# Output-projection pieces, decode tokens and the value projection of the memory, reordered in a two-layer hybrid decoder step

## The chip, the cores and the metric

The kernel runs on one core of one Trainium2 chip. The metric is the device time of one execution in microseconds. The median of three runs before the change is 2929.29 us (2924.08, 2929.29 and 9859.3).

## The reference, cut to what matters

Two layers, each for 1024 prompt tokens and for 8 samples of 4 new tokens (32 decode tokens, 4096 cached positions per sample). All in float32.

```
u, cq, ckv, kpe, gq, gk, gv, ga, go = split(rmsnorm(x) @ w_in)
ya = pool_mixer(u)                                   # 256 columns of the mix
yb = mla_attend(q_lat, q_pe, ckv, kpe) @ w_uv        # 512: prompt causal; decode over pages + new tokens
# GLA, chunk by chunk, 4 heads, key width 32, value width 64
S  = exp(b_last) * S + einsum('bhsk,bhsv->bhkv', kb * exp(b_last - b), vb)   # one state per sample and head
yc = rmsnorm(o, g_gla) * silu(go)                    # 256
x  = x + concat(ya, yb, yc) @ w_out
mem_n = rmsnorm(mem_prompt, g_mem); mk = mem_n @ w_xk; mv = mem_n @ w_xv     # 256 memory tokens
x  = x + cross_attn(rmsnorm(x, g_x), mk, mv)
x  = x + hier_moe(rmsnorm(x, g_ffn))
```

The outputs are the activations, the new latents and keys, the pool buffers, the GLA states of the prompt and of each sample (head by head, so only the blocks of 32 x 64 in which a head's keys meet the same head's values), and mk and mv.

## The kernel before

The five engines run programs of their own, written out by hand in one order each, and meet through semaphores; nothing is scheduled. x lies feature-major in SBUF: 8 tiles of 128 features by 1056 tokens (1024 + 32), worked on in three chunks of 352 tokens. A layer is a sequence of stages with a barrier of four engines behind each (`stage_end`, L433): 2 (input projection, pool, MLA of the prompt), 3 (GLA), 4 (decode attention over the cached pages), 5 (output projection), 9 (cross attention and routing), then the experts and the sum of their outputs. A float32 matmul leaves two records in the trace.

**GLA (stage 3).** Prompt chunks of 128 tokens, n = 0 to 7. On TensorE, `levels(n)` (L882, small matmuls into banks 0 to 3) waits until DVE has taken chunk n-1 out of those banks and GpSimd has made the factors; then come `turn_kt`, `outputs` and `states` of the chunk before. DVE's `take_levels` is seven predicated copies (L1987) and one product; then it adds the state (L2009, a product with the block mask, and L2010), takes the output, begins chunk n+2 (a scan and seven subtractions, L1973 and L1977), and for odd n norms two chunks (`norm_o`, L2001 to L2005). ScalarE takes exponentials for chunk n+2 and the roots of the norms (`roots_of`); exponential and root are in different tables, and each change is an ACT_TABLE_LOAD.

**Pieces.** `part(i)` (L928) is a piece of the output projection that needs no GLA output: the first 6 of 8 contraction tiles of output tile j, chunk c, from `PART`, into bank 5, which DVE's `add_part` adds to x. Chunk 2 holds decode tokens and is left out. PART has five of the eight such pieces. The three others are done whole in the gaps at the end of stage 4 by `project` (L1021, 8 matmuls each, at L1086, L1095 and L1113).

**Decode tokens of GLA.** Behind the loop DVE norms the last two prompt chunks, then prepares the 32 decode tokens (L2048 to L2071, with ScalarE's exponentials L1572 to L1575 between). TensorE then makes their attention (L956), outputs (L966, L968) and eight states (L977), which alternate between banks 7 and 5; DVE adds each by two instructions, a product with the block mask (`bdmask`) and the update.

**Decode attention (stage 4).** At its start TensorE multiplies queries with the keys of the new tokens (L988 to L992: a transpose and 16 small matmuls), DVE takes their maxima (L2100 to L2107) and ScalarE the exponential (L1600). Then sample by sample: GpSimd gathers the cache rows into three slots; TensorE transposes them four blocks at a time through banks 0 and 1, which ScalarE (L1591) and DVE (L2113) empty in turn, and makes scores (L1031, L1038); DVE takes the maximum (L2118), ScalarE the exponential (L1596); the probabilities are transposed and multiplied with the values (L1055) inside the next sample. Behind sample 7 stands a chain of small steps that puts the shares together (L1090 to L1116).

**Stage 5 and behind.** `linear` (L666) runs the output projection, DVE adds each tile to x (L2180), ScalarE squares it (L1399), DVE sums the squares (L2188). Behind the barrier: the sum over partitions (L656), ScalarE's roots (L1405), DVE's norm (L1791, L1793); meanwhile TensorE projects the memory to values (L1136) and keys (L1143), and then makes the queries (L666 again).

## Time and profile before

| | |
|---|---|
| median of the runs | 2929.29 us |
| the profiled execution's own time | 2909.44 us |
| its span | 2907.6 us |
| PE busy (matmul records) | 2629.3 us, 90% |
| DVE, ACT, POOL busy | 1181.6, 721.1, 413.6 us |
| chain: PE, DVE, ACT | 80%, 11%, 4% |
| L935, first and second layer, records | 120 |
| stage 3, first layer | about 437 to 549 us |
| stage 4 | 549 to 692 us |
| stage 5 | 692.5 to 782 us |

Busy time counts an engine's instructions, overlapped or not with others. The chain is followed back from the last instruction to what released it, so that only its members can shorten the run. In a timeline row the two first numbers are the start and the length of a group in microseconds, x is the number of records, and a bracket gives the idle time of the engine ahead of it and what ended it. Where a clock is given, 1.00 is TensorE at 2.4 GHz and 0.50 at 1.2 GHz.

### The profile page before, as it was taken

The numbers are of one execution on the slowest core, as the hardware profiler recorded it, in microseconds if no ns is written. First come the engines' busy times: TensorE is split into PE (matmuls) and PEld (weight loads), VectorE is DVE, ScalarE is ACT, GpSimd is POOL, SyncE is SP. The second block draws the span as 40 slices with busy tenths as digits, with TensorE's granted clock in tenths as the row PEclk, the third lists the DMA queues.
The fourth block names the chain that finished last, engine by engine and source line by source line (L and its number), as shares of the span: only waits on it lengthen the run. The fifth ranks groups of instructions, "written<-read, shape, count | busy, mean of one in ns | idle before, by whom it ended". The sixth has DMA issues, their size and how long they took to land.

```text
span 2907.6 us, 39018 instructions
## 1 busy us (share of the span) xinstructions
PE 2629.3 (90%) x15964; PEld 1837.8 (63%) x15964; DVE 1181.6 (41%) x2218; ACT 721.1 (25%) x1448; POOL 413.6 (14%) x561
## 2 busy tenths in 40 slices
PE   7999987899999979999699999788999997999993
PEld 4645556556567568888465455565666665888872
DVE  4155558442313433232352555574323234323325
ACT  1124453331003301111301344443211132111113
POOL 0004216110000011111100223241000000111111
PEclk9999997799999989999799999968999997999996
DMA  4001001342042268898510100114222313889854
GB/s 160 17 17 32 6 4 34 116 179 73 29 137 98 99 223 325 323 336 321 193 38 4 37 11 8 34 38 152 106 87 98 108 44 139 307 317 334 331 211 181
DMA packets 76933, 385.65 MB, mean 133 GB/s; under 512 B 25087, under 2 KB 31869, under 8 KB 65725
## 3 DMA queue, kind: packets, MB, share of 16 engines
q1 hardware_dynamic: 53164, 304.90, 28.8%
q0 software_dynamic: 23040, 76.59, 7.5%
q8 instruction: 100, 1.64, 0.2%
q10 hardware_dynamic: 576, 2.10, 0.2%
q14 instruction: 53, 0.43, 0.0%
HBM read 355.55 MB, written 44.55 MB: 138 GB/s over the span
## 4 chain that ended last, share of the span: by engine, by line
PE 80%; DVE 11%; ACT 4%; DMA 1%; issue 1%; POOLq 1%; POOL 1%; SPq 0%; DVEq 0%; ACTq 0%
PE ps L666 17%; PE ps L1314 16%; PE ps L1327 8%; PE ps L1232 4%; PE ps L724 4%; PE ps L804 4%; PE ps L816 2%; PE ps L1000 2%; PE ps L832 2%; PE ps L1303 2%; PE ps L782 2%; DVE arena L1987 2%; PE ps L1025 1%; PE ps L1038 1%; DVE nmax L1888 1%
## 5 line engine op out<-in xcount | busy, mean ns | idle before, releaser
L666 PE MATMUL ps<-arena,ring 128*128 128x352 f32 x1704 | 505.8, 459 | 3.4 <-DVE arena L1777 2.4
L1314 PEld LDWEIGHTS ps<-arena 128*128 128x128 f32 x4096 | 470.4, 193 | 35.7 <-issue 35.7
L1314 PE MATMUL ps<-arena 128*128 128x104 f32 x4096 | 470.0, 276 | 4.9 <-issue 2.5
L666 PEld LDWEIGHTS ps<-arena,ring 128*128 128x128 f32 x1704 | 323.4, 190 | 183.6 <-issue 3.5
L1327 PE MATMUL ps<-arena 128*104 128x512 f32 x512 | 230.4, 593 | 2.6 <-ACT arena L1707 2.6
L1707 ACT ACTIVATE arena<-ps 104x1024 f32<-104x1024 f32 x64 | 65.6, 1024 | 470.7 <-PE ps L1327 470.7
L2408 DVE TENSOR_SCALAR arena<-arena 128x208 f32<-128x208 f32 x64 | 17.2, 269 | 400.8 <-ACT arena L1700 400.8
L2543 POOL DMA_INDIRECT arena<-xrow,arena x64 | 70.5, 1102 | 671.8 <-PE ps L1303 353.2
L1327 PEld LDWEIGHTS ps<-arena 128*104 128x104 f32 x512 | 81.9, 170 | 103.9 <-issue 103.9
L804 PE MATMUL ps<-arena 96*128 96x512 f32 (+3 forms) x384 | 146.1, 490 | 0.0
L1232 PE MATMUL ps<-arena,ring 128*128 128x352 f32 x384 | 117.7, 463 | 1.6 <-DVE arena L2258 1.6
L1476 ACT ACTIVATE ring<-ps 128x512 f32<-128x512 f32 (+2 forms) x192 | 87.3, 490 | 124.8 <-PE ps L816 124.7
L1000 PE MATMUL ps<-consts,arena 128*128 128x128 f32 x640 | 99.5, 295 | 19.0 <-ACT arena L1591 12.7
L724 PE MATMUL ps<-arena 128*128 128x512 f32 x256 | 111.2, 593 | 4.5 <-ACT arena L1427 4.5
L816 PE MATMUL ps<-consts,ring 128*128 128x128 f32 x576 | 89.7, 283 | 24.7 <-DVE arena L1899 9.7
L1481 ACT ACTIVATE ring<-ps,nmax 128x128 f32<-128x128 f32 (+7 forms) x128 | 94.6, 741 | 53.5 <-DVE nmax L1889 52.9
L1000 PEld LDWEIGHTS ps<-consts,arena 128*128 128x128 f32 x640 | 74.3, 148 | 49.0 <-ACT arena L1591 23.9
L2549 POOL DMA_INDIRECT yrow<-arena x64 | 65.2, 1018 | 266.7 <-ACT arena L1707 252.5
L1232 PEld LDWEIGHTS ps<-arena,ring 128*128 128x128 f32 x384 | 71.7, 190 | 46.1 <-issue 6.8
L816 PEld LDWEIGHTS ps<-consts,ring 128*128 128x128 f32 x576 | 64.2, 142 | 57.2 <-issue 33.9
L1888 DVE TENSOR_REDUCE nmax<-ps 128x1 f32<-128x128 f32 (+7 forms) x128 | 97.0, 758 | 4.4
L1887 DVE TENSOR_TENSOR ps<-ps,consts 128x128 f32<-128x128 f32 x128 | 38.3, 299 | 146.3 <-PE ps L804 145.4
(410 smaller groups left out, 3649.1 us busy)
## 6 DMA issues: line engine op xcount, KB each, us to landing
arena<-in_w_e SPq DMA_DIRECT2D x64, 3072.0 KB, 13.8
ring<-in_ring SPq DMA_DIRECT2D x56, 512.0 KB, 3.5
arena<-yrow SPq DMA_DIRECT2D x16, 1024.0 KB, 7.9
arena<-in_mem_k SPq DMA_DIRECT2D x16, 512.0 KB, 6.4
arena<-in_mem_v SPq DMA_DIRECT2D x16, 512.0 KB, 10.0
xrow<-arena SPq DMA_DIRECT2D x16, 512.0 KB, 6.4
x<-in_x SPq DMA_DIRECT2D x3, 1408.0 KB, 11.8
out_y<-arena SPq DMA_DIRECT2D x3, 1408.0 KB, 5.6
```

The source lines that it names most:

```text
L666: mm = pe.matmul(ps[:, (j % 2) * NCH + c, 0:CH], ring[:, j // per, (j % per) * units + k, :], src[:, k, tok], start=k == k0, stop=k == uni ...
L724: mm = pe.matmul(ps[:, 6 + t % 2, :], xn[:, k, t * P:t * P + m], wvg[:, k, :], start=k == 0, stop=k == KT - 1)
L804: mm = pe.matmul(ps[:, bank + at // 512, 0:end - at], q_h[0:QK, b, qb * P:(qb + 1) * P], k_h[0:QK, b, at:end], start=True, stop=True)
L816: mm = pe.transpose(ps[:, bank, (kb % 4) * P:(kb % 4 + 1) * P], prob[:, e, kb * P:(kb + 1) * P], ident)
L1000: mm = pe.transpose(ps[:, turn_bank(u), j * P:(j + 1) * P], b, ident)
L1232: mm = pe.matmul(ps[:, (j % 2) * NCH + c, 0:CH], ring[:, slot, (j % 2) * XH + k, :], co[:, k, tok], start=k == 0, stop=k == XH - 1)
L1314: mm = pe.matmul((gate_ps if m < 2 else up_ps)[:, m % 2, 0:rows], w_e[j][:, at:at + P], xb_t[:, p, k, 0:rows], start=k == 0, stop=k == KT - 1)
L1327: mm = pe.matmul(ps[0:rows, 4 + f, :], h_t[:, p, k, 0:rows], w_e[j][:, at:at + 512], start=k == 0, stop=k == 1)
L1476: act.activation(pt[:, e, 512 * half:512 * half + w], ps[:, 4 + m % 2, 0:w], ACT.Copy).then_inc(tp_free[m % 2], 1)
L1481: act.activation(prob[:, e, 0:w], ps[:, 2 * e:2 * e + 2, :].rearrange("p a n -> p (a n)")[:, 0:w], ACT.Exp, bias=nmax[:, e, 1:2], scale=ML ...
L1888: step(dve.reduce_max(nmax[:, e, 0:1], sc, AX))
L2543: pool.indirect_dma_start(xb[0:rows, n % 2, :], None, xrow, bass.IndirectOffsetOnAxis(ap=idx[0:rows, 0, n:n + 1], axis=0), bounds_check=TO ...
```

## The change

Six edits, made in each layer:

- PART has eight pieces instead of five. Their place in the loop is behind `states(n)` for n = 1 to 5; the last stands behind the loop. `project` in stage 4 starts at contraction tile 6.
- The eight decode states use six banks in turn, and DVE adds each by one instruction, without the product with the block mask. What then stands outside the heads' blocks is not read by anything.
- DVE's two last norms stand behind the decode tokens' preparation, and ScalarE's root for them behind the decode exponentials.
- The new tokens' scores (`new_scores`), their maxima (`new_maxima`) and exponential move from the start of stage 4 behind sample 0's scores, into sample 1.
- The value projection of the memory moves from behind the sums of squares to ahead of barrier 5.
- TensorE's wait for the new tokens' maxima (`tail_dve` at 3) moves ahead of the transposes of sample 0's probabilities.

```diff
-PART = ((1, 1), (2, 0), (2, 1), (3, 0), (3, 1))
+PART = ((1, 1), (1, 0), (2, 0), (2, 1), (3, 0), (3, 1), (0, 0), (0, 1))
 PART_K = 6
+STATE_BANKS = (7, 5, 0, 1, 2, 3)
...
                     states(n)
-                    if n in (1, 3):
-                        part(2 + n // 2)
+                    if 1 <= n <= len(PART) - 3:
+                        part(1 + n)
...
-                part(4)
+                part(len(PART) - 1)
...
-                    if b >= 2:
-                        pe.wait_ge(st_ready, NT + 1 + b - 1)
-                    pe.matmul(ps[:, 7 - 2 * (b % 2), 0:GW], d_kt[0:ND, b, :], vg[0:ND, NT, 0:GW],
+                    if b >= len(STATE_BANKS):
+                        pe.wait_ge(st_ready, NT + 1 + b + 1 - len(STATE_BANKS))
+                    pe.matmul(ps[:, STATE_BANKS[b % len(STATE_BANKS)], 0:GW], d_kt[0:ND, b, :], vg[0:ND, NT, 0:GW],
...
-                pe.wait_ge(tail_dve, 1)
-                pe.transpose(ps[:, 3, 0:P], ckv_rep.rearrange("p r k -> p (r k)"), ident).then_inc(tail_pe, 1)
-                for n in range(DB):
...
+                def new_scores():
+
+                    pe.wait_ge(tail_dve, 1)
+                    pe.transpose(ps[:, 3, 0:P], ckv_rep.rearrange("p r k -> p (r k)"), ident).then_inc(tail_pe, 1)
+                    for n in range(DB):
+                        out = ps[0:ND, 7, n * ND:(n + 1) * ND]
+                        pe.matmul(out, q_dec[:, n, :], ckv_new, start=True, stop=False)
+                        mm = pe.matmul(out, qpe_new[64:96, n, :], kr_new[64:96, :], start=False, stop=True)
+                    mm.then_inc(tail_pe, 1)
...
-                    for k in range(KT):
-                        pe.matmul(ps[:, j * NCH + c, 0:CH], ring[:, j, k, :], mix[:, k, chunks[c][1]], start=k == 0, stop=k == KT - 1)
+                    for k in range(PART_K, KT):
+                        pe.matmul(ps[:, j * NCH + c, 0:CH], ring[:, j, k, :], mix[:, k, chunks[c][1]], start=k == PART_K, stop=k == KT - 1)
...
+                    if n == 1:
+                        pe.wait_ge(tail_dve, 3)
                     if n >= 1:
                         up = u
                         turn_probs(n - 1, up)
...
                     rope_scores(n, 1, False).then_inc(sc_done, 1)
+                    if n == 0:
+                        new_scores()
...
                 linear(1, IN_MT + RING, 3, mix)
-                stage_end(pe, 5)
-
-                pe.wait_ge(sq_added, 1)
-                sum_squares(lambda k, c: sq[:, 0, chunks[c][1]], None, 1, NCH, 0, sq_ready, ssq_ready)
                 pe.wait_ge(mnorm_ready, 1)
                 pe.wait_ge(wxv_full, 16)
                 for t in range(2):
...
                     mm.then_inc(mv_done, 1)
+                stage_end(pe, 5)
+
+                pe.wait_ge(sq_added, 1)
+                sum_squares(lambda k, c: sq[:, 0, chunks[c][1]], None, 1, NCH, 0, sq_ready, ssq_ready)
...
-                roots_of(P, 2)
                 act.wait_ge(g_sub, NT + 1)
...
                 act.activation(g_last[:, 0, :], g_b[:, 0, 0:ND].rearrange("p (b t) -> p b t", b=DB)[:, :, DT - 1], ACT.Exp).then_inc(g_exp, 1)
+                roots_of(P, 2)
...
                         take_turn(u, ct[:, h, 0:4, :].rearrange("p b k -> p (b k)"))
+                        if h == 0 and n == 1:
+                            act.wait_ge(tail_dve, 3)
+                            act.activation(p_new[0:ND], p_new[0:ND], ACT.Exp, scale=MLA_SCALE).then_inc(pd_ready, 1)
                         if h == 0 and n >= 1:
                             probs(n - 1)
...
-                    if n in (2, 4):
-                        add_part(1 + n // 2)
+                    if 2 <= n <= len(PART) - 2:
+                        add_part(n)
...
                 take_o(NT - 1)
-                norm_o(NT - 2, P)
-                norm_o(NT - 1, P)
...
-                add_part(4)
+                add_part(len(PART) - 1)
+                norm_o(NT - 2, P)
+                norm_o(NT - 1, P)
...
                     dve.wait_ge(st_done, NT + b + 1)
-                    dve.wait_ge(st_ready, NT + b + 1)
-                    add_state(d_state[:, b, :], 7 - 2 * (b % 2), g_last[:, 0, b:b + 1])
+                    dve.scalar_tensor_tensor(out=d_state[:, b, :], in0=d_state[:, b, :], scalar=g_last[:, 0, b:b + 1],
+                                             in1=ps[:, STATE_BANKS[b % len(STATE_BANKS)], 0:GW], op0=ALU.mult,
+                                             op1=ALU.add).then_inc(st_ready, 1)
...
                     if n >= 1:
                         maxima(n - 1)
+                    if n == 1:
+                        new_maxima()
```

How the order of instructions changes is shown at three places; the line numbers of the changed kernel are 1 to 5 higher. On TensorE in the GLA loop, behind a chunk without a piece before (L893 is `levels`, L907 to L909 `outputs`, L916 `states`, L935 a piece):

```order
L893 MATMUL ps<-arena 128x64 x28
L894 MATMUL ps<-consts,arena 128x4
L900 MATMUL ps<-consts,arena 128x128
L907 MATMUL ps<-arena 128x256
L909 MATMUL ps<-arena 128x64 x4
L916 MATMUL ps<-arena 128x256
L893 MATMUL ps<-arena 128x64 x28
```

and in the change:

```order
L894 MATMUL ps<-arena 128x64 x28
L895 MATMUL ps<-consts,arena 128x4
L901 MATMUL ps<-consts,arena 128x128
L908 MATMUL ps<-arena 128x256
L910 MATMUL ps<-arena 128x64 x4
L917 MATMUL ps<-arena 128x256
L936 MATMUL ps<-arena,ring 128x352 x6
L894 MATMUL ps<-arena 128x64 x28
```

A piece stands between the states of one chunk and the levels of the next but one. On TensorE at the start of stage 4 before (L988 and L991, L992 are the new tokens' scores, cut after two of eight pairs in what follows):

```order
L982 MATMUL ps<-consts,arena 128x32 x2
L988 MATMUL ps<-consts,arena 128x128
L991 MATMUL ps<-arena 32x32
L992 MATMUL ps<-arena 32x32
L991 MATMUL ps<-arena 32x32
L992 MATMUL ps<-arena 32x32
```

and in the change, up to the same matmuls:

```order
L983 MATMUL ps<-consts,arena 128x32 x2
L1003 MATMUL ps<-consts,arena 128x128 x16
L1014 MATMUL ps<-consts,arena 128x128 x4
L1003 MATMUL ps<-consts,arena 128x128 x16
L1014 MATMUL ps<-consts,arena 128x128 x4
L1041 MATMUL ps<-arena 128x512
L1034 MATMUL ps<-arena 32x512 x8
L1041 MATMUL ps<-arena 128x512
L991 MATMUL ps<-consts,arena 128x128
L994 MATMUL ps<-arena 32x32
L995 MATMUL ps<-arena 32x32
```

All transposes and scores of sample 0 stand ahead of them now. On TensorE behind decode attention before:

```order
L1025 MATMUL ps<-arena,ring 128x352 x8
L1116 MATMUL ps<-arena 64x32 x8
L666 MATMUL ps<-arena,ring 128x352 x42
L1125 MATMUL ps<-arena,consts 128x256 x8
L666 MATMUL ps<-arena,ring 128x352 x96
L656 MATMUL ps<-arena,consts 128x352 x3
L1136 MATMUL ps<-arena 128x512 x16
L1143 MATMUL ps<-arena,ring 128x256 x32
```

and in the change:

```order
L1028 MATMUL ps<-arena,ring 128x352 x2
L1121 MATMUL ps<-arena 64x32 x8
L667 MATMUL ps<-arena,ring 128x352 x42
L1130 MATMUL ps<-arena,consts 128x256 x8
L667 MATMUL ps<-arena,ring 128x352 x96
L1137 MATMUL ps<-arena 128x512 x16
L657 MATMUL ps<-arena,consts 128x352 x3
L1148 MATMUL ps<-arena,ring 128x256 x32
```

The last block of `project` has two matmuls instead of eight, the output projection keeps its 42 and 96, and the values (L1136, now L1137) stand ahead of the sums of squares (L656, now L657).

## Rows read from the trace of the kernel before

**Rows 1.** The page's chain of waits: share of the span by engine.

```profile
PE 80%; DVE 11%; ACT 4%; DMA 1%; issue 1%; POOLq 1%; POOL 1%; SPq 0%; DVEq 0%; ACTq 0%
```

**Rows 2.** Table by stretches: us, busy (records) per engine, clock, DMA share, GB/s.

```profile
437.00:549.00 112.00, 86.83 (x693) 64.83 (x693) 83.87 (x227) 38.32 (x146) 50.19 (x141) 0.71 0.13 46
...
563.00:564.00 1.00, 1.00 (x10) 1.00 (x10) 0.30 (x1) 0.60 (x1) 0.00 (x0) 0.89 0.88 377
```

**Rows 3.** Timeline of PE in the GLA stage: start, us, what, idle before.

```profile
474.23 1.79 PE L893 MATMUL ps<-arena 32*128 32x64 f32 x56
...
499.94 3.26 PE L893 MATMUL ps<-arena 32*128 32x64 f32 x56 [3.78 <-POOL arena L2505]
...
522.41 3.72 PE L935 MATMUL ps<-arena,ring 128*128 128x352 f32 x12
...
533.74 4.69 PE L966 MATMUL ps<-arena 128*32 128x256 f32 x16
```

**Rows 4.** Timeline of PE, second layer, the decode tokens' first matmuls.

```profile
1957.79 1.49 PE L956 MATMUL ps<-arena 128*32 128x128 f32 x6 [4.92 <-DVE arena L2071]
```

**Rows 5.** Timeline of DVE, the end of the GLA stage.

```profile
512.53 3.83 DVE L1987 COPY_PREDICATED arena<-lmask,ps 128x256 f32<-128x256 uint8 x7 [2.78 <-PE ps L894]
...
525.16 0.18 DVE L2001 RECIPROCAL arena<-arena 128x4 f32<-128x4 f32 x1 [1.95 <-ACT arena L1545]
...
527.18 0.17 DVE L2048 COPY arena<-arena 128x32 f32<-128x32 f32 x1
...
532.59 0.28 DVE L2076 TENSOR_TENSOR arena<-ps,consts 32x128 f32<-32x128 f32 x1 [1.15 <-PE ps L956]
...
548.55 0.48 DVE L2010 SCALAR_TENSOR_TENSOR arena<-arena 128x256 f32<-128x256 f32 x1
```

**Rows 6.** Timeline of ScalarE, decode tokens, and decode attention's start.

```profile
528.59 0.26 ACT L1572 ACTIVATE arena<-arena 128x64 f32<-128x64 f32 x1 [2.15 <-DVE arena L2059]
...
555.30 1.28 ACT L1600 ACT_TABLE_LOAD   x1 [6.73 <-DVE arena L2107]
...
569.35 1.12 ACT L1596 ACTIVATE arena<-ps,arena 128x1024 f32<-128x1024 f32 x1 [0.42 <-DVE arena L2119]
```

**Rows 7.** Timeline of PE, the start of decode attention.

```profile
549.54 0.44 PE L988 MATMUL ps<-consts,arena 128*128 128x128 f32 x1 [1.33 <-DVE arena L2100]
...
557.54 1.97 PE L1000 MATMUL ps<-consts,arena 128*128 128x128 f32 x8 [1.76 <-ACT arena L1591]
...
567.70 1.04 PE L1000 MATMUL ps<-consts,arena 128*128 128x128 f32 x8
...
571.19 1.06 PE L1000 MATMUL ps<-consts,arena 128*128 128x128 f32 x8
...
580.93 1.04 PE L1000 MATMUL ps<-consts,arena 128*128 128x128 f32 x8
```

**Rows 8.** GpSimd's load for sample 1, and DMA issues from 549 to 570.

```profile
553.10 0.94 POOL L2514 DMA_INDIRECT arena<-in_cache_ckv,page_i  x1 [37.22 <-DMA out_gla_s<-arena]
...
arena<-in_cache_ckv,page_i POOLq DMA_INDIRECT x2, 10.4
```

**Rows 9.** Timeline of PE, end of decode attention, start of the output projection.

```profile
660.26 4.90 PE L1025 MATMUL ps<-arena,ring 128*128 128x352 f32 x16
...
683.50 7.96 PE L1025 MATMUL ps<-arena,ring 128*128 128x352 f32 x16
...
692.54 25.12 PE L666 MATMUL ps<-arena,ring 128*128 128x352 f32 x84 [0.49 <-ACTq L435]
```

**Rows 10.** PE behind the output projection, and DVE's last norm there.

```profile
781.89 3.59 PE L656 MATMUL ps<-arena,consts 128*128 128x352 f32 x6 [3.99 <-DVEq L435]
785.32 13.90 PE L1136 MATMUL ps<-arena 128*128 128x512 f32 x32
...
812.86 22.35 PE L666 MATMUL ps<-arena,ring 128*128 128x352 f32 x75
...
799.16 4.06 DVE L1793 SCALAR_TENSOR_TENSOR arena<-x,vec,arena 128x352 f32<-128x352 f32 x8
```

More of the change, by code:

```diff
@@ L984, in _ @@
                 stage_end(pe, 3)
-                pe.wait_ge(tail_dve, 1)
-                pe.transpose(ps[:, 3, 0:P], ckv_rep.rearrange("p r k -> p (r k)"), ident).then_inc(tail_pe, 1)
-                for n in range(DB):
-                    out = ps[0:ND, 7, n * ND:(n + 1) * ND]
-                    pe.matmul(out, q_dec[:, n, :], ckv_new, start=True, stop=False)
-                    mm = pe.matmul(out, qpe_new[64:96, n, :], kr_new[64:96, :], start=False, stop=True)
-                mm.then_inc(tail_pe, 1)
+                def new_scores():
[6 more added lines that the diff above has]
+                    mm.then_inc(tail_pe, 1)
                 def ring_turns(u, blocks):
@@ L1075, in _ @@
                     latent_scores(n, 0, False)
-                    if n == 1:
-                        pe.wait_ge(tail_dve, 3)
                     if n >= 1:
@@ L2089, in _ @@
                 for b in range(DB):
-                    if b == 3:
+                    if b == 5:
                         norm_o(NT, ND)
                     dve.wait_ge(st_done, NT + b + 1)
-                    dve.wait_ge(st_ready, NT + b + 1)
-                    add_state(d_state[:, b, :], 7 - 2 * (b % 2), g_last[:, 0, b:b + 1])
+                    dve.scalar_tensor_tensor(out=d_state[:, b, :], in0=d_state[:, b, :], scalar=g_last[:, 0, b:b + 1],
+                                             in1=ps[:, STATE_BANKS[b % len(STATE_BANKS)], 0:GW], op0=ALU.mult,
+                                             op1=ALU.add).then_inc(st_ready, 1)
                 step.sync()
@@ L2100, in _, with new_maxima @@
                 dve.tensor_copy(ckv_rep, ckv_new.unsqueeze(1).broadcast_to([P, 4, ND])).then_inc(tail_dve, 1)
-                dve.wait_ge(tail_pe, 1)
-                dve.tensor_copy(ckv_tok, ps[:, 3, 0:P]).then_inc(tail_dve, 1)
-                dve.wait_ge(tail_pe, 2)
-                step(dve.tensor_tensor(p_new[0:ND], ps[0:ND, 7, 0:DB * ND].rearrange("p (b k) -> p b k", b=DB),
-                                       con("newmask", ND).rearrange("p (b k) -> p b k", b=DB), ALU.add))
-                step(dve.tensor_reduce(m_new[0:ND, :], p_new[0:ND], AX, ALU.max))
-                dve.tensor_tensor(p_new[0:ND], p_new[0:ND], m_new[0:ND, :].unsqueeze(2).broadcast_to([ND, DB, ND]),
-                                  ALU.subtract).then_inc(tail_dve, 1)
+                def new_maxima():
+                    dve.wait_ge(tail_pe, 1)
+                    dve.tensor_copy(ckv_tok, ps[:, 3, 0:P]).then_inc(tail_dve, 1)
+                    dve.wait_ge(tail_pe, 2)
+                    step(dve.tensor_tensor(p_new[0:ND], ps[0:ND, 7, 0:DB * ND].rearrange("p (b k) -> p b k", b=DB),
+                                           con("newmask", ND).rearrange("p (b k) -> p b k", b=DB), ALU.add))
+                    step(dve.tensor_reduce(m_new[0:ND, :], p_new[0:ND], AX, ALU.max))
+                    dve.tensor_tensor(p_new[0:ND], p_new[0:ND], m_new[0:ND, :].unsqueeze(2).broadcast_to([ND, DB, ND]),
+                                      ALU.subtract).then_inc(tail_dve, 1)
                 def take_turn(u, dst):
```

2 lines of the change are left out of this document (removed).

## Prediction

> **What bounds the kernel now.** I began with the page: TensorE (PE) holds 80% of the chain that ended last and DVE 11% [rows 1], so a microsecond is won only where PE waits, or where PE does work on the chain that could stand in one of its waits. Then I took a table by stretches and the timeline of each engine around the moved pieces. The GLA stage (437 to 549 us) keeps PE busy for 86.83 of its 112 us, at a mean clock of 0.71 of full speed [rows 2]: room for more matmuls. The reader should see two prices of the same instructions: 56 small records take 1.79 us at the high clock and 3.26 us at the low one [rows 3]. (A matmul leaves two records in the trace, so a piece of six matmuls is x12.) The second layer repeats the first 1426.73 us later: its wait of 4.92 us ahead of L956 [rows 4] has the place and the size of the first layer's. So I cost one layer and double it.
>
> **1. Three more pieces in the GLA loop.** Each is x12 records, 3.72 us at the high clock [rows 3]; before, they were the first six of eight matmuls in the three blocks at L1025. Piece 1+n now stands behind states(n), for n = 1 to 5, and its bank is free only once DVE has added the piece before it, at the end of DVE's own step n. So a piece starts just as DVE begins its seven predicated copies (3.83 us [rows 5]), during which PE has nothing else to do, since levels(n+2) waits for those copies and the bias product behind them. 3.72 us beside 3.83 + 0.42 us: hidden, at the high clock. At the low clock a piece takes some 7 us and shows 2.7 us past the cover. What the pieces fill is the gap of 3.78 us ahead of levels(6) [rows 3], and fuller work should keep the clock up, which is worth 1.5 us at levels(7), for which DVE waits 2.78 us [rows 5]. The three extra adds on DVE (0.5 us each) stand ahead of that wait. I take -0.5 us; ends -2 and +9.
>
> **2. The decode tokens' end of the GLA stage.** DVE was free at 525.16 - 1.95 = 523.2 us but prepared the decode tokens only at 527.18, after two norms [rows 5]. Now it starts at 523.2. ScalarE had its table loaded by 528.59 - 2.15 = 526.4 and then waited 2.15 us for DVE [rows 6]; that wait goes, and the decode products come 2.2 us earlier. The norms (2.0 us for two, from 525.16 to 527.18) now stand behind them, ahead of the read at 532.59, which had 1.15 us of idle time: that read comes 2.2 - 2.0 + 1.15 = 1.3 us earlier. Then the eight states. Before, DVE did sixteen operations and a norm from 539.0 to 549.0, in step with PE over two banks. Now eight operations of 0.48 us [rows 5], a norm of 1.0 and PE's sixteen records, which at 0.29 to 0.43 us each (4.69 us for sixteen of this width between the two clocks [rows 3]) take 4.7 to 6.9 us: 6.4 us in place of 10.0. Together -1.3 - 3.6 = -4.9 us; ends -3 and -6.
>
> **3. The new tokens' scores, from the start of decode attention to behind sample 0.** They occupy PE from 549.54 to 557.54 - 1.76 - 1.97 = 553.81 us, that is 4.3 us, and behind them ScalarE's table load and exponential hold up its first copy by 1.6 us (from 555.30 to 556.9, the end of PE's wait at 557.54 less the copy's own 0.6) [rows 6, 7]. Both go: -5.9 us. But sample 1 gets them back. Between its first transpose (567.70) and the transposes of sample 0's probabilities (571.19) lie 3.5 us now [rows 7]. After the change this is 4.3 us of small matmuls, 1.5 us of DVE (553.81 to 555.30), 1.6 us of table load and exponential, and the 1.8 us from ScalarE's large exponential at 569.35 to 571.19 [rows 6]: 9.2 us, +5.7. Nothing covers it, since DVE's and ScalarE's copies of sample 1 are queued behind those waits. Besides, the tiny matmuls and the wait should drop the clock, as the 32-column matmuls of step 4 do, behind which dense ones start at the low clock; eight transpose records take 1.97 us low against 1.06 high [rows 7], so 4 us of dense work at the low clock cost 2 us more. The cover on the other side is thin as well: sample 1's cache rows are asked for at 553.10 and take 10.4 us to land [rows 8], 563.5 at best, while PE will want them some 0.2 + 12.3 + 4.3 us after the stage's start, at 566. Sum +2 us; ends -1 and +6.
>
> The same row on table loads bears on a page. The trace shows 1.28 us and the exponential right behind it [rows 6]. The Trainium skill ("ScalarE: Activation LUTs", What ACT_TABLE_LOAD costs) adds a drain and gives about 2.66 us for each switch; by that, sample 1 would lose 1.4 us more in each layer. The trace disagrees, and I keep its number.
>
> **4. The end of decode attention.** The blocks at L1025 shrink from x16 to x4. The first (4.90 us at 660.26) covered DVE's maximum and ScalarE's exponential; at sample 0 that exponential starts 1.65 us behind the last scores' records and takes 1.3 [rows 6, 7], so the next PE work is ready at about 663.2 instead of 665.0: -1.8. The second, as long, becomes 1.2: the copy it covers is ready by then, -3.6. The third (683.50) takes 7.96 us, which is eleven records at the low price of 0.587 and five at the high one of 0.293: four cost 2.35, -5.6 [rows 9]. Against these: before, this block brought the clock back 6.5 us in, so that the output projection at 692.54 ran at 0.30 us a record from its first one (25.12 us for x84 [rows 9]). Now it starts some 3.5 us after 683.5 and runs low for 3 to 6 us: +2.3, with the ends 1.5 and 3.3. The small matmuls ahead may be cold for longer: +0.5. Sum -8.2 us; ends -11 and -5. The projection itself has as many matmuls as before.
>
> **5. The value projection ahead of the barrier.** PE idles 3.99 us there while DVE adds the last tile and two squares, then runs the sums of squares at the low clock, 3.59 us for x6 [rows 10]; at 0.293 a record they need 1.8. With the 13.90 us of values in front, the others finish first, and PE passes the barrier in about the 0.49 us that the last one took [rows 9]: -3.5 - 1.8. What the values covered is uncovered: the roots on ScalarE, 0.7 us of wait ahead of the key projection, and DVE's norm, which now ends behind the barrier by the same 19 us, at about 812. The key projection (14 us) covers its first chunks, and the query projection wants the third chunk only after four tiles of 4.7 us. DVE ended at 803.2 before, with PE ready for it at 812.9: a slack of 10 us, and enough is left [rows 10]. Sum -4.6 us; ends -5.8 and -3.
>
> **The sum.** -0.5 - 4.9 + 2.0 - 8.2 - 4.6 = -16.2 us a layer, -32 for both. The profiled execution's own time is 2909.4 us (span 2907.6), so its like would be 2877. The runs' median lies 20 us above it, at 2929.3 (two runs within 5 us of each other, the third an outlier): I forecast 2897 us.
>
> **The rivals.**
> (a) *The pieces run at the low clock* and each of the four behind the second shows 3 us past DVE's copies: +12.5 us a layer, 2922 us. For it: levels(6) at 499.94 already runs low [rows 3]. Against: each piece is the densest work there is in the loop. 0.12.
> (b) *Sample 1 lengthens more*: the low clock lasts over all of it, and its cache rows land late. A sample lasts 13.2 us at the high clock (567.70 to 580.93, the same for the next ones); at the transposes' ratio of 1.97 to 1.06 it would take 10 us more, so +8 on my term: 2913 us. 0.10.
> (c) *The clock stays high through the GLA stage*, and the decode tokens' end gains by it too: every term at its better end gives -26 a layer, 2878 us. 0.10.
> (d) *The clock does not come back in decode attention*: slower. All but the first samples cost 10 us more each, and beyond 1.6 samples a layer at the low clock the gain is gone; with seven it is -16 + 70 a layer, some 3037 us. For it would speak that transposes come first in each sample. Against: between 553.81 and 563.9 PE did nothing but transposes, and the clock rose in 563 to 564 (0.89 [rows 2]). 0.02. The Trainium skill ("TensorE: Matmul & The Clock Gate", Part 4: PE-mode transpose) says that transposes do not count as busy for the clock; the trace here disagrees, as that rise shows.
> My forecast has the other 0.66. That the moves are undone by another order is no case: the order of instructions shows each of them.
>
> **How the numbers follow.** The range 2866 to 2918 holds the forecast with its terms between the ends, (b) and (c), and allows for runs at the profiled level instead of 20 us above it; (d) and part of (a) are outside. Faster by over 2% (about what a measurement can tell from no change) means below 2870.7: only (c) on a good run, 0.05. Slower by over 2% is (d), 0.02. Within 2%: 0.93.
>
> **What would show it.** Right, in the changed profile: the last set of predicated copies of a layer's loop starting no later than 512.5; the stage's end near 544; PE transposing at once in the next stage, then a wait of 4 us or more in sample 1 released by ScalarE, at a clock below 1.00; blocks of x4; the sums of squares at 1.8 us behind a gap under 1 us. Wrong: predicated copies waiting for PE in each step of the GLA loop (step 1), a gap at sample 1 ended by a DMA (step 3), the output projection taking over 29 us for its x84 (step 4), or a wait for DVE at the query projection (step 5).

## The result and the profile after

| | before | changed |
|---|---|---|
| median of the runs shown, us | 2926.68 (4 runs, one an outlier of 9859) | 2875.54 (4 runs, 2866.96 to 2883.03) |
| profiled execution's own time, us | 2909.44 | 2866.96 |
| its span, us; mean granted clock | 2907.6; 0.94 | 2865.1; 0.952 |
| PE busy (matmul records), us | 2629.3 | 2605.3 |

The ratio is 0.9834, 95% interval [0.9801, 0.9868]: 1.7% faster, within the 2% called no change. A second set of runs on one chip gave 0.9848 [0.9823, 0.9874]. The forecast was 2897; the range 2866 to 2918 held the result, but the gain was larger than its sum.

A ledger of both layers comes first. Each column is the time between two starts on TensorE's timeline: first piece of the GLA stage, first cache transposes of decode attention, first shortened block at its end (L1025 before, L1028 now), output projection's first tile, memory's squares, query projection.

| us, layer 1 / layer 2 | before | changed | difference |
|---|---|---|---|
| A first piece to transposes | 112.5 / 112.7 | 101.4 / 101.6 | -11.1 / -11.1 |
| B transposes to end block | 106.5 / 106.5 | 108.9 / 108.1 | +2.5 / +1.6 |
| C end block to output projection | 32.3 / 32.3 | 22.0 / 21.8 | -10.3 / -10.5 |
| D first tiles of the projection | 25.0 / 25.0 | 27.6 / 25.0 | +2.7 / 0.0 |
| E memory's squares to queries | 95.4 / 95.4 | 90.9 / 90.9 | -4.5 / -4.5 |
| sum | 371.6 / 371.8 | 350.8 / 347.3 | -20.8 / -24.5 |

The two sums give 45.2 us, and the spans differ by 42.5: everything outside these stretches takes 2164.3 us before and 2167.0 after. So the gain is where the edits are.

The table by stretches shows the clock [rows 2]. Columns: stretch, its length, busy us and records of PE, PEld, DVE, ACT and POOL, granted clock, DMA share, GB/s.

```profile
443.75:545.00 101.25, 85.53 (x729) 61.90 (x729) 77.32 (x206) 36.79 (x143) 46.59 (x139) 0.85 0.13 42
545.00:549.00 4.00, 3.87 (x20) 3.40 (x21) 1.17 (x4) 1.19 (x2) 0.00 (x0) 0.58 0.31 66
549.00:555.00 6.00, 5.87 (x41) 3.05 (x40) 2.45 (x4) 1.79 (x3) 3.75 (x4) 1.00 0.72 254
...
559.00:563.00 4.00, 3.51 (x16) 3.05 (x17) 1.74 (x4) 2.33 (x4) 0.00 (x0) 0.50 0.96 409
```

The GLA stage has a mean clock of 0.85, where the same stretch (441.30 to 549.17) had 0.72. The clock falls to 0.50 as decode attention starts and is at 1.00 from 549 us on; taken by single microseconds the clock came back 3.2 us after the first transposes. Before, those started at 553.81 and it came in 563 to 564, 9.4 us after them.

PE in the GLA loop, answering to [rows 3]: the pieces behind states(2) to states(5), of which the first, third and fourth stand where there was none before, and levels(6):

```profile
480.35 3.71 PE L936 MATMUL ps<-arena,ring 128*128 128x352 f32 x12
...
489.12 3.79 PE L936 MATMUL ps<-arena,ring 128*128 128x352 f32 x12 [0.53 <-DVE x L2023]
...
498.69 3.71 PE L936 MATMUL ps<-arena,ring 128*128 128x352 f32 x12
502.65 1.79 PE L894 MATMUL ps<-arena 32*128 32x64 f32 x56 [0.24 <-POOL arena L2516]
...
507.62 3.79 PE L936 MATMUL ps<-arena,ring 128*128 128x352 f32 x12 [0.53 <-DVE x L2023]
```

levels(6) waits 0.24 us instead of 3.78 and runs at the high clock. DVE's timeline at the end of the stage [rows 5], the last row being the first of the next stage:

```profile
513.99 3.84 DVE L1993 COPY_PREDICATED arena<-lmask,ps 128x256 f32<-128x256 uint8 x7 [0.67 <-PE ps L895]
...
524.60 0.17 DVE L2052 COPY arena<-arena 128x32 f32<-128x32 f32 x1
...
532.59 0.27 DVE L2082 TENSOR_TENSOR arena<-ps,consts 32x128 f32<-32x128 f32 x1
...
540.68 2.21 DVE L2099 SCALAR_TENSOR_TENSOR arena<-arena,ps 128x256 f32<-128x256 f32 x5 [0.21 <-PE ps L978]
...
545.16 0.23 DVE L2107 COPY arena<-arena 128x128 f32<-128x128 f32 x1
```

and ScalarE's, for the decode tokens' exponentials [rows 6]:

```profile
526.52 1.28 ACT L1576 ACT_TABLE_LOAD   x1
527.81 0.26 ACT L1576 ACTIVATE arena<-arena 128x64 f32<-128x64 f32 x1
```

The stage began 2.45 us later here (443.75 for 441.30), so from its start the copies come 1.0 us earlier, the read of the products 2.45, and L2107 6.46. Five states go through in 2.21 us without a wait between them. That they are five comes of an edit which the list of changes leaves out: the decode tokens' own norm moved from behind the third state to behind the fifth. It belongs to the decode tokens' part, and no run separates it from the states. The exponential now follows its table load at once.

PE in decode attention [rows 7]:

```profile
545.13 3.61 PE L1003 MATMUL ps<-consts,arena 128*128 128x128 f32 x16 [0.91 <-DVEq L436]
...
549.01 2.60 PE L1003 MATMUL ps<-consts,arena 128*128 128x128 f32 x16
...
555.66 0.27 PE L991 MATMUL ps<-consts,arena 128*128 128x128 f32 x1
555.86 0.25 PE L994 MATMUL ps<-arena 128*32 128x32 f32 x2
556.04 0.24 PE L995 MATMUL ps<-arena 32*32 32x32 f32 x2
...
559.49 3.87 PE L1003 MATMUL ps<-consts,arena 128*128 128x128 f32 x16 [0.70 <-DMA arena<-in_cache_kpe,page_i]
...
564.67 1.41 PE L1003 MATMUL ps<-consts,arena 128*128 128x128 f32 x8 [0.46 <-ACT arena L1596]
```

Sample 0 has no wait and lasts 10.5 us; the new scores (555.66) take 3.1 us at the high clock; sample 1 then meets its cache rows 0.70 us before they land. ScalarE there:

```profile
560.64 0.60 ACT L1596 ACTIVATE arena<-ps 128x512 f32<-128x512 f32 x1 [7.95 <-PE ps L1003]
561.25 1.28 ACT L1610 ACT_TABLE_LOAD   x1
562.55 0.41 ACT L1610 ACTIVATE arena<-arena 32x256 f32<-32x256 f32 x1
562.87 1.09 ACT L1601 ACTIVATE arena<-ps,arena 128x1024 f32<-128x1024 f32 x1
```

PE at the end of decode attention and at barrier 5 [rows 9, 10]; the row at 2081.21 is the second layer's projection:

```profile
654.06 1.35 PE L1028 MATMUL ps<-arena,ring 128*128 128x352 f32 x4
656.97 0.27 PE L1095 MATMUL ps<-consts,arena 128*8 128x128 f32 x1 [1.56 <-ACT arena L1601]
...
658.54 1.35 PE L1028 MATMUL ps<-arena,ring 128*128 128x352 f32 x4
...
671.81 2.71 PE L1028 MATMUL ps<-arena,ring 128*128 128x352 f32 x4
...
676.01 27.80 PE L667 MATMUL ps<-arena,ring 128*128 128x352 f32 x84 [0.49 <-ACTq L436]
...
763.90 13.90 PE L1137 MATMUL ps<-arena 128*128 128x512 f32 x32
778.06 2.01 PE L657 MATMUL ps<-arena,consts 128*128 128x352 f32 x6 [0.26 <-PEq L436]
780.63 14.08 PE L1148 MATMUL ps<-arena,ring 128*128 128x256 f32 x64 [0.55 <-ACT arena L1410]
...
2081.21 25.12 PE L667 MATMUL ps<-arena,ring 128*128 128x352 f32 x84 [0.49 <-ACTq L436]
```

### The profile page after: what moved, and what is told of

It reads as the page before. It is cut to its first block, busy times and chain, and to the rows that moved or that the text cites. A ratio compares the mean times of both kernels' runs of the same rounds, so it can differ in the third digit from the quotient of the medians.

```text
span 2865.1 us, 38998 instructions
## 1 busy us (share of the span) xinstructions
PE 2605.3 (91%) x15964; PEld 1817.8 (63%) x15964; DVE 1176.1 (41%) x2208; ACT 720.4 (25%) x1448; POOL 413.7 (14%) x561
## 4 chain that ended last, share of the span: by engine, by line
PE 73%; DVE 10%; PEld 4%; ACT 4%; issue 4%; DMA 2%; POOLq 1%; POOL 1%; PEldq 1%; SPq 0%; DVEq 0%; ACTq 0%
PE ps L1319 16%; PE ps L667 12%; PE ps L1332 8%; PE ps L1237 4%; PE ps L725 4%; PE ps L805 4%; PEld ps L667 4%; PE ps L817 2%; PE ps L833 2%; PE ps L1003 2%; PE ps L1308 2%; PE ps L783 2%; DVE arena L1993 1%; DVE nmax L1894 1%; PE ps L936 1%
## 5 line engine op out<-in xcount | busy, mean ns | idle before, releaser
L1003 PE MATMUL ps<-consts,arena 128*128 128x128 f32 x640 | 99.9, 296 | 18.7 <-ACT arena L1596 10.4
L1003 PEld LDWEIGHTS ps<-consts,arena 128*128 128x128 f32 x640 | 73.9, 149 | 48.6 <-ACT arena L1596 19.9
```

The costliest lines, as they stand in the source:

```text
L1003: mm = pe.transpose(ps[:, turn_bank(u), j * P:(j + 1) * P], b, ident)
```

## The experiments

Twelve runs followed, of eleven kernels, each against the kernel before on the same chip; the third column counts the two layers' sums of the ledger against before (743.3 us).

| kernel | ratio to before, 95% | ledger, us |
|---|---|---|
| e1_values: before + value projection | 0.9947 [0.9924, 0.9971] | -10.9 |
| e2_scores: before + scores' move | 0.9991 [0.9971, 1.001] | -5.2 |
| e3_pieces: before + eight pieces | 0.9943 [0.9923, 0.9962] | -16.0 |
| e4_decode: before + decode tokens | 0.9954 [0.9933, 0.9975] | -15.8 |
| c_change: the change again | 0.9848 [0.9823, 0.9874] | -43.5 |
| u2_no_scores: change less scores' move | 0.9888 [0.9864, 0.9913] | -40.3 |
| u3_no_pieces: change less pieces | 0.9900 [0.9882, 0.9918] | -27.8 |
| d1_norms: before + half of e4 | 0.9996 [0.9983, 1.001] | -6.2 |
| x_double: change, pieces twice | 0.9966 [0.995, 0.9982] | -16.1 |
| i1_preload: change + early table load | 0.9857 [0.9829, 0.9886] | -50.9 |
| i1_again: the same | 0.9848 [0.9827, 0.9868] | -51.0 |
| i2_late_scores: i1 + scores behind sample 2 | 0.9857 [0.9828, 0.9886] | -41.1 |

**My theory** was that each part saves in its own place and the savings add. **The rival** was that they gain from one another through TensorE's clock. Each part was done alone first, its code being its part of the change's diff.

*The value projection alone.*

```diff
-                stage_end(pe, 5)
-
-                pe.wait_ge(sq_added, 1)
-                sum_squares(lambda k, c: sq[:, 0, chunks[c][1]], None, 1, NCH, 0, sq_ready, ssq_ready)
                 pe.wait_ge(mnorm_ready, 1)
...
                     mm.then_inc(mv_done, 1)
+                stage_end(pe, 5)
```

> The kernel before with one part of the change alone: the value projection of the memory ahead of barrier 5. Theory (the parts save separately, each in its own place): of the changed kernel's profile the step from the last output-projection tile to the query projection is 4.3 us shorter per layer, so 8.6 us less in all, about 2921 against 2929 for the kernel before. The clock over the barrier stays as it is there. Rival (the value projection only fills a wait that the later work then shows again, because the keys wait for the norm of the memory or for the sum over the barrier): 0 to 3 us less in all, with a new idle time ahead of the key projection of 3 us or more.

Column E is 90.9 in both layers, -4.5, the whole of what the change has there; the rows are those of the change to 0.01 us (the sums 2.01 us behind 0.26 of waiting). No wait of 3 us appeared at the keys. The median fell by 15.9 us, more than 9: 1.7 us of the rest are in column C of the second layer, and what is left lies outside the ledger. The rival falls.

*The scores' move alone.*

```diff
-                pe.wait_ge(tail_dve, 1)
-                pe.transpose(ps[:, 3, 0:P], ckv_rep.rearrange("p r k -> p (r k)"), ident).then_inc(tail_pe, 1)
...
                     rope_scores(n, 1, False).then_inc(sc_done, 1)
+                    if n == 0:
+                        new_scores()
```

> The kernel before with the new tokens' scores moved into sample 1, and nothing else. Theory A (the clock rises some 4 us after the first transposes, whatever ran before them, as in the changed kernel): sample 0 lasts about 10.5 us instead of 18.5, sample 1 about 19.1 instead of 13.2, so 2.1 us less per layer and 4 us less in all. Theory B (TensorE's sparse work at the end of the GLA stage, which this kernel keeps, holds the clock down longer, about 10 us after the first transposes as in the kernel before): sample 0 lasts 12.6 us or more, so that the edit alone gives nothing or loses up to 2 us per layer: 0 to 4 us more in all, and the gain in the changed kernel came from the two edits together.

Theory A, with the clock of the stage's first eight microseconds as witness:

```profile
548.75:552.75 4.00, 4.00 (x18) 3.53 (x19) 1.02 (x3) 1.20 (x2) 0.05 (x1) 0.50 0.31 66
552.75:556.75 4.00, 3.75 (x26) 2.78 (x24) 2.67 (x4) 1.79 (x3) 3.09 (x4) 0.96 0.61 188
```

The GLA stage ends here as sparsely as before, and still the clock is up 4.3 us after the first transposes (3.9 in the second layer). A and B together are 1.9 and 1.4 us shorter; the rest of the 5.2 is clock in column C (-3.0 and -1.5), against +1.1 and +1.4 in E, where the value projection starts low behind the barrier. The interval holds 1.

*The pieces alone.*

```diff
-PART = ((1, 1), (2, 0), (2, 1), (3, 0), (3, 1))
+PART = ((1, 1), (1, 0), (2, 0), (2, 1), (3, 0), (3, 1), (0, 0), (0, 1))
```

> The kernel before with eight pieces of the output projection in the GLA loop instead of five, and the tail of decode attention shortened by their work; nothing else. Theory (as separate savings): the loop no longer than before (added pieces 3.7 us each, in waits that were there), the tail and the first tile of the output projection about 8 us shorter per layer, 16 us less in all, and the output projection runs cold at its start (2.7 us more in one layer, as in the changed kernel). Rival (the loop gets longer by what the pieces take, 3 times 3.7 us at high clock, and its wait only moves): the tail's gain is eaten by 5 to 11 us per layer, 0 to 8 us less in all. Second rival (the loop is shorter only since the pieces hold the clock up): the loop is 1 us shorter here too, and the levels of turn 6 start at high clock.

In both layers column C is 11.7 us shorter, D 2.7 longer and E 1.2 longer, and column A is 0.3 and 0.5 us shorter: the sum is -16.0 as the theory had it. The second rival holds for its smaller part: levels(6) runs at the high clock (1.79 us) and the last copies come 0.7 us earlier. The mean clock of the stage is 0.82 here (443.24 to 555.00) for 0.72 before, and column A hardly shortens: in this stage TensorE's clock buys little.

*The decode tokens alone.*

```diff
-                    dve.wait_ge(st_ready, NT + b + 1)
-                    add_state(d_state[:, b, :], 7 - 2 * (b % 2), g_last[:, 0, b:b + 1])
+                    dve.scalar_tensor_tensor(out=d_state[:, b, :], in0=d_state[:, b, :], scalar=g_last[:, 0, b:b + 1],
+                                             in1=ps[:, STATE_BANKS[b % len(STATE_BANKS)], 0:GW], op0=ALU.mult,
+                                             op1=ALU.add).then_inc(st_ready, 1)
```

> The kernel before with the decode tokens' part of the GLA stage alone: states without the mask and in six banks, norms of the last two turns behind the decode tokens' factors. Theory (separate savings): the stage ends 5.4 us earlier per layer than before, 11 us less in all. In the stage behind it the clock of TensorE decides a further part: if sparse work at the end of the GLA stage held it down, it rises earlier here and sample 0 is up to 2 us shorter per layer (15 us less in all); if not, sample 0 keeps its 18.5 us. Rival (the norms that were moved become the last to end, so the stage's end is theirs): 1 to 2 us less per layer, 2 to 4 us less in all, with TensorE idle at the stage's end behind the norms.

Column A is 5.8 us shorter, as expected; B is unchanged (106.3), so sample 0 keeps its length; C gives 3.0 more by its clock, and E takes 1.1 back. The 15 us are there, but their second part comes at the other end of decode attention than expected. The rival (the norms end last) falls: DVE's last operations are states, as in the change.

The four ratios add up to 0.53 + 0.09 + 0.57 + 0.46 = 1.65% and the four ledgers to 47.9 us, against 1.52% (and 1.66% in the first set) and 43.5 to 45.2 us for the change.

> The changed kernel once more, with more runs, as the level for the others of this set. Theory (the four parts save separately): the four run alone gave ratios of 0.9947 (value projection), 0.9991 (scores), 0.9943 (pieces) and 0.9954 (decode tokens), which add up to 4.8% less... 0.53 + 0.09 + 0.57 + 0.46 = 1.65%, so a ratio of 0.9835 here, some 48 us less. Rival (they gain from one another through the clock of TensorE): a ratio under 0.980.

(The sum in that text is 1.65%; the "4.8%" in it is a slip for 48 us.) The theory stands: no gain from the parts' meeting is seen, though the intervals would hide one of some 10 us. Inside it the clock's shares do not add, but nearly cancel: the four alone sum to -18 us a layer in column C, where the change has -10, and to -1 in E, where it has -4.5.

*The scores' move, and then the pieces, taken out of the change.*

```diff
+                pe.wait_ge(tail_dve, 1)
+                pe.transpose(ps[:, 3, 0:P], ckv_rep.rearrange("p r k -> p (r k)"), ident).then_inc(tail_pe, 1)
...
-                    if n == 0:
-                        new_scores()
```

> The changed kernel with the new tokens' scores back at the start of decode attention (the other three parts stay). Theory A (the scores' move is worth what it is alone, 1.4 to 1.9 us per layer): 3 to 5 us more in all than the changed kernel; the sample-0 transposes again wait for ScalarE and the clock reaches its high level some 10 us after the first of them. Theory B (the move pays only since the GLA stage now ends at the high clock): here the scores themselves run at the high clock (0.25 us a pair of records, as they do in sample 1 of the changed kernel, instead of 0.32), so the front is 1 us shorter than in the kernel before and the change is worth less here, 0 to 2 us in all.

Ledger +0.6 and +2.6 us, 3.2 in all: the lower end of A (columns A and B alone +2.1 and +2.8). The ratio says more, 0.9888 for 0.9848, some 12 us, with intervals that overlap; what exceeds 3.2 lies outside the ledger and is not explained. The scores at the start run low (0.32 and 0.31 us a pair of records), and the clock comes 8.8 us after the first transposes, which again wait 1.8 us for ScalarE behind its table load. B falls.

```diff
-PART = ((1, 1), (1, 0), (2, 0), (2, 1), (3, 0), (3, 1), (0, 0), (0, 1))
+PART = ((1, 1), (2, 0), (2, 1), (3, 0), (3, 1))
```

> The changed kernel with five pieces instead of eight (the other three parts stay). Theory A (separate savings): 8 us per layer more than the changed kernel (the price that the pieces had alone), a ratio to the kernel before near 0.990, and the last step of the GLA stage at the high clock as in the changed kernel. Theory B (the pieces are what keeps the clock up, so the GLA stage ends at the low clock here): the end of the stage from the last output piece to its barrier is 1 to 2 us longer and the levels of turn 6 run low, but sample 0 of decode attention is as short as in the changed kernel, because its clock rises some 4 us after the first transposes either way: 9 to 10 us per layer more.

+6.0 and +9.8 us, 15.8 in all: A's size. One point of B is true, the levels without a piece ahead of them:

```profile
497.30 3.26 PE L894 MATMUL ps<-arena 32*128 32x64 f32 x56 [3.79 <-POOL arena L2516]
...
535.32 3.72 PE L978 MATMUL ps<-arena 32*128 32x256 f32 x16
```

The stage's last matmuls (535.32, 0.23 us a record) are at the high clock without the pieces as well. And column A is 101.9 and 102.0, only 0.4 longer: 1.47 us of clock on PE and 3.5 us of its waiting are nearly off the path, on which DVE's own work lies.

This run also prices the low clock in sample 1. In its first layer the clock does not fall behind the new scores at all, and column B is still 108.5 us, for 108.9 and 109.1 in the change's two profiles and 106.5 before:

```profile
555.17 1.09 PE L1003 MATMUL ps<-consts,arena 128*128 128x128 f32 x8 [1.14 <-DMA arena<-in_cache_kpe,page_i]
...
559.89 1.07 PE L1003 MATMUL ps<-consts,arena 128*128 128x128 f32 x8 [1.76 <-ACT arena L1596]
```

The transposes run high here, and TensorE waits 1.76 us for ScalarE where the change, at the low clock, waits 0.46.

*How full is the loop?*

```diff
-                    for k in range(PART_K):
+                    for k in tuple(range(PART_K)) * (2 if i >= 2 else 1):
```

> The changed kernel with the last six of the eight pieces computed twice (the second pass overwrites the first with the same values), so each takes 7.4 us instead of 3.7. Theory (a piece is hidden beside DVE's seven predicated copies and its add, 3.83 + 0.42 us, and no more): each of the five in the loop shows 3.2 us, and the last, with 2.34 us of waiting behind it, 1.4 us: 17 us per layer, 35 us in all. Rival (TensorE has slack left in the loop, so that the copies of DVE alone set its pace): under 2 us for each, under 20 us in all. Second rival (the full TensorE shortens nothing and delays ScalarE's and GpSimd's inputs as well): over 45 us in all.

The ratio is 1.18% above the change's, 34 us; the ledger has 11.1 and 16.4 us, of which A 10.5 and 14.4. One step:

```profile
488.53 7.26 PE L936 MATMUL ps<-arena,ring 128*128 128x352 f32 x24
...
500.03 7.26 PE L936 MATMUL ps<-arena,ring 128*128 128x352 f32 x24
```

From piece to piece the loop took 7.92, 8.77, 9.57, 8.93 and 16.39 us in the change (from 472.43, 480.35, 489.12, 498.69 and 507.62 on) and takes 11.07, 11.07, 11.50, 11.06 and 19.78 here (the rows are the third of these steps): of 3.5 us more, 3.2, 2.3, 1.9, 2.1 and 3.4 show. So the pieces nearly fill the cover, with a slack of 0.1 to 1.6 us in a step, which I had not counted. By the ratio the theory's 35 us is right, by the ledger, with 27.4, it is some 8 us too much; the 7 us between ratio and ledger are not explained.

*Half of the decode tokens' part: the order of the norms.*

```diff
-                norm_o(NT - 2, P)
-                norm_o(NT - 1, P)
...
                 add_part(4)
+                norm_o(NT - 2, P)
+                norm_o(NT - 1, P)
```

> The kernel before with one half of the decode tokens' part: the last two norms and their roots behind the decode tokens' factors, the states as before (masked, two banks). Theory (two separate terms, 1.3 us for the order and 3.6 to 4.2 us for the states, of the 5.4 to 6.0 us that both together gave): 1.3 us per layer less up to the start of decode attention, 3 us in all, within what the comparison can tell. Rival (the order gives nothing alone, since the states' chain of DVE and TensorE follows and hides it, or the roots' table load moves onto the path): 0 or up to 1 us more.

Column A -0.8 and -1.0; of the ledger's 6.2 us the rest is clock (it comes 7 us after the first transposes instead of 9.4, and earlier in C). The whole cannot be told from no change. The states' half, which did not run alone, is then worth 5.8 - 0.9 = 4.9 us a layer.

*Two tries to do better.* Both load ScalarE's table in its idle time at the start of decode attention; the second also moves the scores behind sample 2.

```diff
+                act.activation(st_e[0:DB, 0, 0:1], con("ones", DB)[:, 0:1], ACT.Exp)
                 u = 0
...
-                    if n == 0:
+                    if n == 2:
+                        pe.wait_ge(o_kept, 2)
                         new_scores()
```

> The changed kernel with one exponential of 32 values more, into a scratch place, at the start of ScalarE's decode attention, so that the table is loaded in its idle time ahead of sample 0 and not in sample 1. Theory (the load is on sample 1's path): sample 1 shorter by what TensorE waits there for ScalarE, at least the 0.46 us ahead of the second half's transposes, at most the 1.28 us of the load: 0.5 to 1.3 us per layer, 1 to 2.5 us in all. Rival (sample 1 is paced by TensorE at the low clock and by the cache rows, so the load is hidden behind them): nothing, under 0.3 us per layer.

> As the one with the early table load, and with the new tokens' scores behind sample 2 instead of sample 0 (their exponential in sample 3). Theory A (in sample 1 the small matmuls cost more than their own 3.1 us because the cache rows land just then, 0.70 us, and because the clock falls behind them, 1.5 to 2 us on the next transposes): behind sample 2 the rows are there, and the whole costs 3.1 us plus the maxima's wait: samples 0 to 3 together 1 to 2.5 us shorter per layer than in the changed kernel. Theory B (the clock falls behind 32-column matmuls wherever they stand, and the rows of sample 1 are waited for longer now that TensorE comes for them 3 us sooner): TensorE waits some 3.8 us for the rows ahead of sample 1 (0.70 + 3.1), and the fall of the clock behind the scores comes later: together equal or up to 4 us per layer longer.

> The changed kernel with the early table load once more, for its interval. Theory (the local saving of 3 to 4 us per layer between the GLA stage and the query projection is real, and the whole differed since other stages took their clock otherwise): a ratio of 0.982 to 0.984, against 0.985 for the changed kernel. Rival (the saving is given back): 0.985 or more.

i1, ScalarE at the start of the stage (the load stands where it waited 1.77 us before):

```profile
551.22 1.28 ACT L1604 ACT_TABLE_LOAD   x1
552.52 0.20 ACT L1604 ACTIVATE arena<-consts 8x1 f32<-8x1 f32 x1
552.84 0.60 ACT L1596 ACTIVATE arena<-ps 128x512 f32<-128x512 f32 x1
```

Column B became 106.9 and 106.7, -2.2 and -1.3 against the change's second set (109.1, 108.0), and C -1.5, and in the second layer D another -1.6: 7.4 us in all, and 7.5 in the repeat. But the ratios are 0.9857 and 0.9848, not under the change's 0.9848. What the ledger shows is about the width of the interval (0.26%, 7.6 us), so this version is neither shown to be better nor shown to give it back.

i2, PE at sample 1:

```profile
556.06 1.13 PE L1041 MATMUL ps<-arena 128*128 128x512 f32 x2
560.22 3.58 PE L1003 MATMUL ps<-consts,arena 128*128 128x128 f32 x16 [3.03 <-DMA arena<-in_cache_kpe,page_i]
```

Theory B: without the scores there, TensorE waits 3.03 us for the cache rows, and B is 110.3, 3.5 us longer than with the scores behind sample 0. In the change the small matmuls fill a wait that their own removal from the front had opened.

## Why the prediction was nearly right, and where its step 3 failed

**Step 1** (-0.5 for the loop): -1.0. By the clock on the wall the last copies came later (513.99) than the 512.5 that I had named as the sign; the sign should have been counted from the stage's start, which moved by 2.45 us for reasons outside. The pieces take the 3.7 us that was forecast, at the high clock, and the gap ahead of levels(6) closed. For the bad end of +9, pieces at the low clock, x_double has the nearest thing, 7.26 us a piece at the high clock: six of them added 10.5 and 14.4 us, 1.8 and 2.4 each where the bad end took 2.7. That the three added pieces cost nothing is shown by u3_no_pieces: without them column A is 0.4 us longer, not shorter.

**Step 2** (-4.9): -5.5. Its three parts measure as worked out: the decode products 3.4 us earlier from the stage's start (530.29 - 443.75 = 86.54, for 1957.79 - 1867.86 = 89.93), of which 1.0 is step 1's; the read -1.45 for -1.3; the states -4.0 for -3.6, at 3.72 us for PE's sixteen records, better than the 4.7 to 6.9 assumed.

**Step 3** (+2) failed: A and B less the 6.46 and 6.39 us of steps 1 and 2 give -2.2 and -3.1. Two of its terms were mis-sized.

The first is the front, worked out as -5.9 from the scores and ScalarE's first copy alone. Counted from DVE's first copy of the stage, it gave 8.0 us (sample 0's scores end 18.5 us behind it before, 10.5 now), because the clock came earlier as well: 3.2 us after the first transposes instead of 9.4. The scores' move is what brings this, since e2_scores alone has it and u2_no_scores has it not. But it takes away two things together, the small matmuls ahead of the transposes and the wait of 1.76 us between them, and no run separates the two.

The second is the clock term of sample 1, +2 ("the tiny matmuls and the wait should drop the clock"). The sample lengthened by 5.9 us, where 5.7 and 2 had been added. The stretch from the new scores to the probabilities' transposes took 9.0 us (555.66 to 564.67) for 9.2, so the 5.7 came out. The clock did fall (0.50 in 559 to 563), but on transposes inside that stretch, where I had put a wait of 4 us for ScalarE; behind 564.67 it cost 0.35 us (10.09 to the next sample, for 9.74 before). The longest wait for ScalarE was 0.46 us, and 1.21 in the second layer. There the clock stayed low for less long, which goes with the 1 us between -2.2 and -3.1. Where it did not fall at all (u3_no_pieces, first layer) column B was 0.5 to 0.6 us shorter than in the change.

The scores' move alone (e2) shows -1.9 and -1.4, so it is this edit's own doing. A sign that I had named for being wrong came too, a gap at sample 1 ended by a DMA, of 0.70 us. The rows landed when forecast, 14.3 us behind DVE's first copy (559.49 - 545.16, for 563.5 - 549.17), but TensorE came for them after 13.6 us, not 16.8, so the slack of 2.5 us was gone; that the scores stand ahead of it kept the wait so small (i2).

**Step 4** (-8.2): -7.6 and -10.5. By terms in the first layer: from the first block to L1095 2.91 us for 4.74 (-1.8 as forecast), the second -3.55 for -3.6, the third 2.71 for 7.96 (-5.3 for -5.6), the cold start of the projection +2.7 for +2.3. In the second layer the clock was back as the projection began and the cold start cost nothing; in the second profile of the change it cost 1.6 us there, so this differs from one execution to the next.

**Step 5** (-4.6): -4.5, with the forecast slack: the keys wait 0.55 us, and the queries wait for nobody.

**The sum** was 32 us where the profiled executions show 42.5. Of the ledger's 45.2, step 3 accounts for 9.3 of the missing 12.8, steps 1 and 2 for 2.1, and the second layer's warm start of the projection for the rest. The forecast of 2897 lies 21.5 us above the measured 2875.5: 10 from these terms, and 11.4 from the 20 us by which I set the median above the profiled execution. That distance was no property of the kernel: before, a set of 31 runs has a median of 2922.5, 13 above the profile; the change's two medians lie 8.6 above and 0.5 under the profiles of their own sets. Stages that no edit touched move by that much from one execution to the next: the GLA stage of layer 1 starts anywhere from 438.2 to 449.9 us in the fourteen traces. A profiled execution is one draw of this.

**The rivals.** (a) did not happen: no added piece ran low. (b) had the right place and the wrong sign. (c) is nearest to what was seen, 24.5 a layer in the second layer; its clock in the GLA loop was the least part of it. (d) did not happen: the clock rose behind nothing but transposes. The Trainium skill ("TensorE: Matmul & The Clock Gate", Part 4: PE-mode transpose) has transposes not count as busy for the clock; between 545.13 and 551.5 us TensorE ran only the transposes of L1003 and L1014, and the clock went from 0.50 to 1.00 there, so this trace disagrees again, now with float32 transposes that no other work interrupts.

## What to carry to other kernels

Cost a move at both of its places, and look there at what the clock does: here the front gained 2.1 us beyond the work that left it. Ask also which transfer the moved work used to hide or hides now. And make the ledger of the stretches that an edit touches, for both kernels and each layer: it told 1 us apart where medians could not tell 7.

## What was not expected of the hardware

- At the start of decode attention, in both layers of the fourteen traces, the granted clock went from 0.50 to 1.00 while TensorE did nothing but transposes. Where these came first and unbroken, it took 3.0 to 4.3 us in fifteen of sixteen cases, with the clock at 1.00 shortly before (the change) or at 0.50 (e2), and 6.0 us in one (x_double, second layer). Where the small matmuls stood ahead and a wait of 1.8 us broke the transposes, it took 6.8 to 9.8 us in all twelve (9.4 before).
- Behind the same sixteen small matmuls the clock fell 3 us after their start in the change, and in u3_no_pieces only 6 us after it in the second layer and not in the first (1.00 for the 29 us behind their start).
- A doubled piece, 3.5 us more of matmuls in a step, showed 1.9 to 3.4 us.
- Repeats of one kernel agree to 0.2 us a layer inside the ledger (i1 and i1_again: 347.8 and 347.7, 344.7 and 344.6), and differ by 11.6 us outside it (2175.4 and 2163.8).
